# The prompt's gate product by one level of Strassen's method, its results leaving in half rows

## What is computed

```
gate = sigmoid((rms_norm(h, norm_ple) @ w_ple_gate) + b_ple_gate)     # 1024 -> 1024
y    = h + gate * (p @ w_ple)
```

## Time and profile before

| | us |
|---|---|
| median of 3 runs | 944.28 (943.15 to 944.61) |
| the profiled execution, device time | 950.47 |
| its span, first to last instruction | 948.6 |
| PE busy in it | 924.1 (97%) |
| DVE busy | 573.8 (60%) |
| ACT busy | 195.3 (21%) |
| mean granted TensorE clock | 0.995 |

### The profile page before, as it was taken

The page is one execution under the profiler, slowest core; times in us unless marked ns, Lnnn a source line. Parts: engine busy times, 40 slices in busy tenths (PEclk is TensorE's granted clock), DMA queues, the critical chain, the costliest instruction groups (busy, mean ns, idle before and its releaser), DMA issues.

```text
span 948.6 us, 11392 instructions
## 1 busy us (share of the span) xinstructions
PE 924.1 (97%) x4417; PEld 467.7 (49%) x4417; DVE 573.8 (60%) x1152; ACT 195.3 (21%) x428; POOL 62.1 (7%) x70
## 2 busy tenths in 40 slices
PE   9999998999999999999999999999999999999997
PEld 5565766887554444634343343434334333334443
DVE  3106430536876693663777787787787675768434
ACT  3111210002746311511111111111111111111401
POOL 3100050000000000010000000000000000000000
PEclk9999998999999999999999999999999999999999
DMA  8690352340001795869999999999999999999311
GB/s 301 213 309 0 108 170 67 126 156 2 1 1 32 189 366 227 321 248 407 420 418 420 420 419 418 419 419 418 420 418 420 419 419 419 418 422 405 115 44 50
DMA packets 74875, 260.58 MB, mean 275 GB/s; under 512 B 12554, under 2 KB 36502, under 8 KB 49956
## 3 DMA queue, kind: packets, MB, share of 16 engines
q1 hardware_dynamic: 69568, 248.51, 67.4%
q0 software_dynamic: 4080, 8.93, 2.8%
q10 hardware_dynamic: 1172, 2.40, 0.7%
HBM read 252.72 MB, written 13.08 MB: 280 GB/s over the span
## 4 chain that ended last, share of the span: by engine, by line
PE 79%; SPq 13%; DMA 4%; DVE 2%; issue 1%; ACT 0%; POOLq 0%; DVEq 0%
PE ps L1164 72%; SPq L386 13%; DMA w<-in_w_exp_down 3%; PE ps L1545 2%; PE ps L1814 1%; PE ps L1188 1%; PE ps L1849 1%; PE ps L1199 0%; DMA xg<-hn_rows,sidx 0%; DMA gmix<-in_norm_mix 0%; PE ps L1548 0%; PE ps L1285 0%; PE ps L1354 0%; DVE probs L2380 0%; PE ps L1370 0%
## 5 line engine op out<-in xcount | busy, mean ns | idle before, releaser
L1164 PE MATMUL ps<-w,xe 128*64 128x512 f32 x1024 | 228.8, 596 | 8.0 <-DMA w<-in_w_exp_up 7.2
L2775 DVE TENSOR_TENSOR h<-h,ps 128x1024 f32<-128x1024 f32 x120 | 143.1, 1214 | 108.1 <-PE ps L1164 108.0
L1164 PEld LDWEIGHTS ps<-w,xe 128*64 128x64 f32 x1024 | 69.8, 137 | 148.0 <-issue 132.4
L1164 PE MATMUL ps<-w,hT 128*64 128x512 f32 x504 | 115.4, 599 | 0.6 <-DMA w<-in_w_exp_down 0.6
L1164 PE MATMUL ps<-yk,ST 128*128 128x512 f32 (+1 forms) x320 | 105.3, 431 | 0.7 <-DVE yk L2765 0.5
L1164 PE MATMUL ps<-xT,wring 128*128 128x272 f32 x384 | 101.5, 405 | 0.0
L1164 PEld LDWEIGHTS ps<-xT,wring 128*128 128x128 f32 x384 | 69.5, 192 | 25.6 <-issue 12.6
L1164 PE MATMUL ps<-wring,xT 128*32 128x128 f32 (+2 forms) x368 | 77.7, 404 | 0.4 <-DVE xT L2049 0.4
L1164 PEld LDWEIGHTS ps<-yk,ST 128*128 128x128 f32 (+1 forms) x320 | 48.6, 174 | 56.9 <-issue 26.7
L1112 ACT ACTIVATE sg<-ps 64x256 f32<-64x256 f32 x64 | 24.1, 377 | 252.9 <-PE ps L1164 241.7
L795 POOL DMA_INDIRECT xg<-hn_rows,sidx x32 | 32.4, 1014 | 644.4 <-PE ps L1814 368.0
(11 more groups left out here) (371 smaller groups left out, 915.0 us busy)
## 6 DMA issues: line engine op xcount, KB each, us to landing
w<-in_w_exp_gate SPq DMA_DIRECT2D x64, 1024.0 KB, 22.6
w<-in_w_exp_up SPq DMA_DIRECT2D x64, 1024.0 KB, 25.4
w<-in_w_exp_down SPq DMA_DIRECT2D x63, 1024.0 KB, 25.2
wring<-in_w_in SPq DMA_DIRECT2D x12, 512.0 KB, 6.5
wpg<-in_w_ple_gate SPq DMA_DIRECT2D x2, 2048.0 KB, 19.7
biaslines<-blrow SPq DMA_DIRECT2D x1, 2560.0 KB, 10.2
h<-in_x_prompt SPq DMA_DIRECT2D x4, 512.0 KB, 8.3
wring<-in_w_in SPq DMA_DIRECT2D x2, 1024.0 KB, 7.5
```

What stands on the lines that cost most here:

```text
L1164: return nc.tensor.matmul(out, l, r, start=start, stop=stop, skip_group_check=skip)
L2775: TTn(h[0:r, t, :], h[0:r, t, :], both(b, r), ALU.add).then_inc(S["hadd"], 1)
```

## The change

The product of the 512 prompt rows with the 1024 x 1024 gate weights is cut into 2 x 2 blocks: `h11, h12, h21, h22` are 256 rows x 512 inputs of `hpT`, `g11` to `g22` are 512 inputs x 512 outputs of `wpg`. Seven products of half the size in each direction take the place of eight (the variant with 4 sums on each side): `h11*g11`, `h12*g21`, `gs1*gt1`, `gs2*gt2`, `gs3*gt3`, `gs4*g22`, `h22*gt4`. A product is 2 row tiles (r) x 4 chunks = 8 `mm`. The transposed rows of all four tiles now stay in `hpT`. DVE forms four sums of weights (`gt`, 128x2048) and four of rows (`gs`, 128x1024). Product 2 adds onto product 1 in the same PSUM bank, after ACT has copied product 1 out (`first_part`, into `half1`); DVE adds products 6 and 7 to that copy (`half1`, `half2`), forms scaled starting values for six of the eight output blocks from them, and adds the scaled last product to each. The sample's product stands before product 3. The outputs leave as eight blocks of 128x512 (256 KB), each from a buffer of its own, and the sample between them. SP's order changes too: the second half of `wpg` and `bpg` now come ahead of `plo`, which moves behind the wait for `d_done` at 31; the scalar counts on `bpg_in` and `pl_in` go with that.

```diff
-        hq = at("hq", [P, 256], 32 * K)
-        bpgq = at("bpgq", [P, 256], 33 * K)
-        rnq = at("rnq", [P, 1], 34 * K)
-        hpT = at("hpT", [P, 2, DC, P], 40 * K)
-        sgt = at("sgt", [P, 2, D], 94.25 * K)
+        QK = DC // 2
+        hpT = at("hpT", [P, DC, SEQ], 32 * K)
+        gs3, gs1, gs2 = (at(f"gs{n}", [P, QK, 2 * P], off * K) for n, off in ((3, 72), (1, 76), (2, 80)))
+        gt1, gt2, gt3, gt4 = (at(f"gt{n + 1}", [P, QK, 512], (94.25 + 8 * n) * K) for n in range(4))
+        zg = at("zg", [P, 8, 512], 126.25 * K)
         tail, tcur = run_of(142.25 * K)
         plo = tail("plo", [P, TT, D])
         bpg = tail("bpg", [P, D])
+        half2 = at("half2", [P, 2, 512], tcur[0])
...
+        g11, g21 = (wpg[:, 0, k * QK:(k + 1) * QK, :] for k in range(2))
+        g12, g22 = (wpg[:, 1, k * QK:(k + 1) * QK, :] for k in range(2))
+        h11, h12, h21, h22 = (hpT[:, k * QK:(k + 1) * QK, r * 2 * P:(r + 1) * 2 * P] for r in range(2) for k in range(2))
+        GATE = {1: (h11, g11, 4), 2: (h12, g21, 4), 7: (gs3, gt3, 0), 6: (gs2, gt2, 2), 4: (h22, gt4, 0), 5: (gs1, gt1, 6), 3: (gs4, g22, 6)}
+        GATE_DONE = ((1, 0), (2, 0), (1, 1), (2, 1), (7, 0), (7, 1), (6, 0), (6, 1), (4, 0), (4, 1), (5, 0), (5, 1), "s", (3, 0), (3, 1))
+        SUMMED = ("c0a", "c0", "gt3", "c1", "gt1", "c2", "gt2", "c3", "gs3", "gs1", "gs2", "gt4", "cs", "gs4", "free0", "free1")
+        BLOCKS = ((0, 0), (1, 0), (2, 0), (3, 0), (2, 1), (3, 1), "s", (0, 1), (1, 1))
...
-            sp.wait_ge(S["d_done"], NE - 2)
+            sp.wait_ge(S["d_done"], NE - 1)
+            sp.dma_start(wpg[:, 1, :, :], w[:, :, 512:D]).then_inc(S["bpg_in"], 16)
+            sp.dma_start(bpg[:], bcast(a["b_ple_gate"], D)).then_inc(S["pl_in"], 16)
             sp.wait_ge(S["pl_out0"], 16 * 2)
             sp.wait_ge(S["pl_out1"], 16 * 4)
             sp.dma_start(plo[:, 0:TP, :], pl_d.rearrange("(t p) n -> p t n", p=P)).then_inc(S["pl_in"], 16)
             sp.dma_start(plo[:, TP, 0:256], plq_d).then_inc(S["pl_in"], 16)
-            sp.wait_ge(S["d_done"], NE - 1)
-            sp.dma_start(wpg[:, 1, :, :], w[:, :, 512:D]).then_inc(S["bpg_in"], 16)
-            sp.dma_start(bpg[:], bcast(a["b_ple_gate"], D)).then_inc(S["bpg_in"], 16)
             for q in range(4):
                 sp.dma_start(bpgq[NS * q:NS * (q + 1), :], bcast(a["b_ple_gate"][q * 256:(q + 1) * 256], 256)[0:NS, :])\
-                    .then_inc(S["bpg_in"], 16)
+                    .then_inc(S["pl_in"], 16)
...
+            for x in BLOCKS:
+                sp.wait_ge(S["f_o"], block_no(x))
+                if x == "s":
+                    for q in range(2):
+                        sample_rows_out(sp, q)
+                else:
+                    t, k = x
+                    sp.dma_start(o["y_prompt"][t * P:(t + 1) * P, k * 512:(k + 1) * 512], gate_of(x)).then_inc(S["f_out0"], 16)
...
+            def first_part(r):
+                act.wait_ge(S["f_mm"], gated_by(1, r))
+                A(half1[:, r, :], ps[:, 4 + r, :], C).then_inc(S["f_sig"], 1)
+            squares(0)
+            squares(1)
+            squares(2)
+            first_part(0)
+            squares(3)
+            first_part(1)
+            squares(TP)
+            for x in BLOCKS:
+                act.wait_ge(S["f_z"], block_no(x))
+                A(gate_of(x), gate_of(x), ACT.Sigmoid).then_inc(S["f_sig"], 1)
+                if x != "s" and block_no(x) == block_no("s") + 1:
+                    act.wait_ge(S["f_o"], block_no("s"))
+                    for q in range(2, 4):
+                        sample_rows_out(act, q)
...
-                pe.wait_ge(S["fin"], (1, 3, TT + 1, TT + 1, TT + 1)[t])
+                pe.wait_ge(S["fin"], (1, 3, 3, TP, TT + 1)[t])
                 if t >= 2:
-                    pe.wait_ge(S["f_hpT"], t)
-                token_T(t, h[0:rows(t), t, :], tail_bank(t), S["f_tr"])
+                    pe.wait_ge(S["f_hpT"], made(("c0", "c1", "c2")[t - 2]))
+                token_T(t, h[0:rows(t), t, :], 2 if t % 2 else 6, S["f_tr"])
...
+            def gate_part(m, r):
+                x, w, b = GATE[m]
+                for c in range(QK):
+                    last = mm(ps[:, b + r, :], x[:, c, r * P:(r + 1) * P], w[:, c, :], c == 0 and m not in (2, 3), c == QK - 1, True)
+                last.then_inc(S["f_mm"], 1)
             final_T(0)
-            for t in range(TT):
-                r, b = rows(t), 4 + 2 * (t % 2)
-                pe.wait_ge(S["f_hpT"], t + 2 if t else 1)
-                if t >= 2:
-                    pe.wait_ge(S["f_z"], t - 1)
-                if t == TP:
-                    quarters(b, hpT[:, t % 2, :, 0:NS], (wpg[:, 0, :, :], wpg[:, 1, :, :])).then_inc(S["f_mm"], 1)
-                    break
-                for half in range(2):
-                    if t == 0:
-                        pe.wait_ge(S[("wpg_in", "bpg_in")[half]], (32, 16 * 7)[half])
-                    for c in range(DC):
-                        if t == half == 0 and c == DC // 2:
-                            pe.wait_ge(S["f_hpT"], 2)
-                        last = mm(ps[0:r, b + half, :], hpT[:, t % 2, c, 0:r], wpg[:, half, c, :],
-                                  c == 0, c == DC - 1)
-                    if half == 0:
-                        if t == TP - 1:
-                            last.then_inc(S["f_mm"], 1)
-                        if t == 0:
-                            sample_sums()
-                        final_T(t + 1)
-                last.then_inc(S["f_mm"], 1)
+            pe.wait_ge(S["wpg_in"], 32)
+            pe.wait_ge(S["fin"], 2)
+            pe.wait_ge(S["f_hpT"], made("c0a"))
+            gate_part(1, 0)
+            final_T(1)
+            pe.wait_ge(S["f_hpT"], made("c0"))
+            pe.wait_ge(S["f_sig"], 1)
+            gate_part(2, 0)
+            final_T(2)
+            pe.wait_ge(S["f_hpT"], made("c1"))
+            gate_part(1, 1)
+            sample_sums()
+            final_T(3)
+            pe.wait_ge(S["f_sig"], 2)
+            gate_part(2, 1)
+            final_T(TP)
+            pe.wait_ge(S["f_hpT"], made("gs3", "gt3"))
+            for r in range(2):
+                gate_part(7, r)
+            pe.wait_ge(S["f_hpT"], made("gs2", "gt2"))
+            for r in range(2):
+                gate_part(6, r)
+            for r in range(2):
+                pe.wait_ge(S["f_hpT"], made("gt4", f"free{r}"))
+                gate_part(4, r)
+            for r in range(2):
+                gate_part(5, r)
+            pe.wait_ge(S["f_z"], block_no((0, 0)))
+            quarters(4, hpTs[:], (wpg[:, 0, :, :], wpg[:, 1, :, :])).then_inc(S["f_mm"], 1)
+            for r in range(2):
+                pe.wait_ge(S["f_z"], block_no((2 + r, 1)))
+                gate_part(3, r)
...
+            def sum_of(name, to, x, y, sign):
+                dve.wait_ge(S["f_hpT"], made(name) - 1)
+                TTn(to, x, y, sign).then_inc(S["f_hpT"], 1)
             for t in range(TP):
                 dve.wait_ge(S["comb"], (L - 1) * NU + 3 * (t + 1))
                 last_add(t, S["fin"], 1)
                 if t == 1:
                     columns(0)
-            rms(rn[:, 0:1])
+            dve.wait_ge(S["wpg_in"], 32)
+            dve.wait_ge(S["bpg_in"], 16 * 2)
+            sum_of("gt3", gt3[:], g22, g12, ALU.subtract)
+            columns(1)
+            sum_of("gt1", gt1[:], g12, g11, ALU.subtract)
+            columns(2)
+            sum_of("gt2", gt2[:], g22, gt1[:], ALU.subtract)
             dve.wait_ge(S["fin"], TT)
             last_add(TP, S["fin"], 1)
-            columns(1)
-            dve.wait_ge(S["bpg_in"], 16 * 7)
-            dve.wait_ge(S["pl_in"], 32)
-            def out_of(n, gate, embed, rest):
-                dve.wait_ge(S["f_sig"], n)
-                chain(TTn(gate, gate, embed, ALU.mult))
-                TTn(gate, gate, rest, ALU.add).then_inc(S["f_o"], 1)
-            for t in range(TP - 1):
-                gate = sgt[:, t % 2, :]
-                if t >= 2:
-                    dve.wait_ge(S[f"f_out{t % 2}"], 16 * (t // 2))
-                dve.wait_ge(S["f_mm"], t + 1)
-                STT(gate, both(4 + 2 * (t % 2)), rn[:, t:t + 1], bpg[:], ALU.mult, ALU.add).then_inc(S["f_z"], 1)
-                if t == 0:
-                    dve.wait_ge(S["root_ok"], len(roots) + TP)
-                    chain(V.reciprocal(rn[:, 1:TP], rn[:, 1:TP]))
-                    chain(V.reciprocal(rn[0:NS, TP:TT], rn[0:NS, TP:TT]))
-                    for q in range(4):
-                        V.tensor_copy(rnq[NS * q:NS * (q + 1), :], rn[0:NS, TP:TT])
-                        V.tensor_copy(hq[NS * q:NS * (q + 1), :], h[0:NS, TP, q * 256:(q + 1) * 256])
-                if t + 2 < TP:
-                    columns(t + 2)
-                out_of(t + 1, gate, plo[:, t, :], h[:, t, :])
-            t = TP - 1
-            dve.wait_ge(S[f"f_out{t % 2}"], 16)
-            for k in range(2):
-                cols = slice(k * 512, (k + 1) * 512)
```

(75 more changed lines are left out.)

50 lines of the change are left out of this document (22 added, 28 removed).

## The result

| | before | changed |
|---|---|---|
| median of the runs, us | 943.3 (942.8 to 944.6) | 937.5 (936.9 to 938.9) |
| ratio, 95% interval | | 0.9934 (0.9924 to 0.9945) |
| profiled execution, device time | 950.47 | 936.85 |
| its span | 948.6 | 935.0 |
| PE busy | 924.1 (97%) | 915.1 (98%) |

The changed kernel is 0.66% faster, 6.2 us of 943.3 by the ratio (5.2 to 7.2) and 5.8 by the medians. The forecast was 5.7 less, and 938.6 for the median; the median is 937.5. The three runs of before that the forecast started from had a median of 944.28, and the six here have 943.3.

A forecast was written before the change was run, and what follows sets the result against it. PE was taken to bound the gate stage: 6.87 us of removed mm, less 0.1 for the copy and about 1.1 for the tail, saves 5.7, so 944.28 - 5.7 = 938.6 us; range 936.8 to 941.3.

The forecast's parts named there:

- Bound and removal: Gate stage after the last expert: PE's list sets the end; 8 of 64 mm at 0.859 us removed, 6.87 us less.
- The pieces: PE's gate list: 14 pieces replace 8 halves, nearly each behind a wait; at most 1.4 us extra, taken as zero.
- The rival of small waits: Gate stage: piece costs, late wpg, the copy or product 4's slack eat part of the gain; about 941 us, chance 0.14.
- ACT's copy: Between products 1 and 2: copy out of PSUM takes 0.60 us, hidden by tile 1's transposes; 0.1 us stall, 0.9 uncovered.
- DVE: Gate stage: weight sums 2.28 us and row sums 1.22, four each, 14.0 us in all, fitting beside PE's work.
- The slack at product 4: DVE frees product 4's two PSUM banks 1.7 and 1.4 us before PE wants them.
- The slower rival: DVE's sums take longer while PE reads the same tiles; at double length PE waits 11.3 us, 949.9 us; chance 0.03.
- The clock: PE in the gate stage: stays at the upper level; rival, half speed for one product, 945.5 us, chance 0.02.
- the DVE rival: Gate stage: DVE becomes the bound through slower sums, 949.9 us at double length; chance 0.03.
- SP's order: SP's loads: second half of wpg lands 12.9 us after issue, plo later by 900.8; cost nothing, up to 1 us.
- The tail: After PE's last piece: 3.17 us on engines, 256 KB DMA 2.0; about 1.1 us of the saving lost here.
- From the profile to the median: Whole time: the 5.7 us saving applies alike to profiled 950.47, giving 944.8, and to median 944.28, giving 938.6.

The follow-up runs named there:

- the first experiment: Kernel before the change with the last of 8 chunks left out of every prompt tile's gate product (8 mm fewer): median 936.98 us, ratio 0.9929, stage 61.47 us.
- The run without the cover: Changed kernel with tile 1's transposes moved behind product 2, so nothing on PE hides ACT's copy of product 1: median 939.85 us, ratio 0.9950, stage 64.07.

## Why the prediction was right, point by point

**Bound and removal.** PE's list set the end of the stage before and sets it after. By the first experiment eight `mm` are worth 6.86 us (6.87 in the sum). In the changed kernel PE's stretch from the first gate record to its last group's end start to start is 49.87 + 6.87 = 56.74 us, against 52.85 + 10.72 = 63.57: 6.83 less. I had 6.87 less the 0.1 of the copy.

**The pieces** cost next to nothing, as I took it. The 0.1 a piece from the output product did not come: 13.83 for two products and 6.96 for one, against 13.74 and 6.87. The rival of small waits had no part in the result.

**ACT's copy.** 0.60, and its stall 0.07 us (the transposes and the gap behind them took 0.95 in place of 0.88), against 0.1. The run without the cover shows that the cover is needed.

**DVE.** 2.29 and 1.2 us for the sums while PE read the same tiles, as in the earlier trace rows. A sum of rows took 1.22 too where PE stood idle (at 894.92 in the run with all sums twice), so there was no contention to see. The slack at product 4 was put at 1.7 and 1.4 and was 1.8 and 1.7; three STT take 2.08, not 2.25. The slower rival's mechanism, sums that take longer beside PE, did not occur. The run with all sums twice stands in for its effect only, and there my price, 11.3 us, was 2.3 too low, because I had let PE's idle stand without what it does to the clock: 2.9 us in product 4. In the prediction the clock was a rival of its own, tied to small pauses between pieces. It belonged to the DVE rival.

**The clock.** In the changed kernel it is 1.00 for as long as PE works in the stage, as I took it, and PE has next to no idle there. In the run with all sums twice it fell within idles of 2.59 and 3.21 us; single idles of 0.78, 1.45 and 2.71 us in three other profiles did not bring it down. The Trainium skill, TensorE: Matmul & The Clock Gate, section "A second HAM failure mode: psum-queue depth-cycling", tells of a kernel whose frequent short idles, as it went through PSUM banks, made the clock swing. The going through all eight banks did not do that here; frequent short idles, the other half of it, this kernel does not have, so the page's case was not tried.

**SP's order.** I costed it at nothing at the old landing of 12.9 us. In the changed kernel's company the old order gave 15.9, and 0.40 us in the stage. Nor did `plo` behave as I had it: `bpg`'s issue ahead of it held the queue for 0.92 us and not 6.60, and `plo` landed at 863.76 + 13.7 = 877.5, more than 18 us ahead of DVE's first gate at 896.12, for which it is waited for; I had 3 us in hand. The step was right in its result and loose in its bound: a landing behind other traffic isn't a constant that one may carry over (12.9, 11.8 and 15.9 in three profiles of the same queue order). Why it was 15.9 was not found.

**The tail.** 3.17 us on the engines as predicted; the last DMA in 2.1 for 2.0. The order with the sample last shows that the 1.0 us that the change doesn't keep is here; the sum had 1.1 for it. The Trainium skill, DMA: Bandwidth & Descriptors, section "Anatomy of one DMA — SWDGE (gpsimd) path", has a fit for DMAs that GpSimd issues, by which 256 KB are an estimated 2.6 us and 512 KB 3.2. SP's DMAs landed in 2.1 and 3.1 here, so the smaller one, on which the sum rested, came out by the row and not by the page.

**From the profile to the median.** I subtracted the stage's gain from the median and let the 6.2 us between profile and median be, without asking what they were; the stretch at 141 us is the likely source. The prediction's figure for the profiled run, 944.8, shows what the question was worth: the changed kernel's profiled run took 936.85. The median came out 1.1 us below the 938.6, and 1.0 of that is the starting point, 944.28 then and 943.3 with three more runs. So the absolute figure says little of the sum; the 5.7 against 5.84 us in the stage is what tests it.

## What to carry to other kernels

- Where PE is the bound of a stage, a removed matmul is worth its start-to-start time, and one level of Strassen's method keeps it if the sums lie on an engine that waits for PE anyway: here 5.8 of 6.9 us. Walk the other engine's list against PE's with the old trace's durations; the slack that came out was right to 0.3 us.
- Where the walk gives PE an idle of some microseconds, add what the clock may take behind it, here 2.9 of 13.65 us. Count it only where PE sets the pace: work that runs slower ahead of a wait for another engine costs nothing until that wait is used up.
- Look at what ends last. Putting the smallest output at the end was worth 1.0 us of the stage, nearly all that the change had not kept of its 6.9.
